# Delta rule of a hybrid transformer block: another way to the triangular inverse, norms by column groups, and work moved between stages

## The chip, the cores and the metric

One core of a Trainium2 chip runs the whole kernel in one launch. The metric is device time in microseconds (us), the median of the runs; for the kernel before it is 1261.51 us over three runs (1257.89 to 1262.75). Engines: PE is the matrix engine (TensorE), DVE the vector engine, ACT the scalar engine, POOL is GpSimd, SP issues the DMAs. They run side by side and wait for each other through semaphores, all written by hand here.

## The reference, cut to what matters

Four layers run one after another: forgetting attention, a gated delta net with a convolutional FFN behind each, then latent attention and block attention. The change concerns the delta net, and there the part between its input projections and its output projection (8 heads of width 128, 272 tokens padded to 3 chunks of C = 96):

```python
q = l2norm(q) * (Dh ** -0.5); k = l2norm(k)
dec = jnp.exp(jnp.where(incl, gc[..., :, None] - gc[..., None, :], -jnp.inf))
A = jnp.where(strict, (kc @ kc.T) * dec * beta, 0.0)
sol = lax.linalg.triangular_solve(A + I, rhs, lower=True, unit_diagonal=True)   # rhs: keys, values
qk = (qc @ kc.T) * dec
def step(S, xs):                      # over the 3 chunks
    U = U0_n - W_n @ S
    O = qd_n @ S + qk_n @ U
    S = gl_n * S + U.T @ kd_n
O = rmsnorm(O, o_gain) * silu(og);  out = O @ w_out
```

The kernel doesn't solve: it builds the inverse D of I + A (96 x 96, lower triangular, one for each of 24 head and chunk pairs) and multiplies by it.

## The kernel before, in words

Weights are split in a high and a low part, and every big product is three matmuls at float32r (L365 to L367). The delta net has these stages.

- Projections (`project`, L1393): for each head d four features, q, k, v and gate. ACT scales them out of PSUM (`tap`), DVE adds three convolution taps (`conv`, L1736), ACT applies silu and squares (`silu_sq`). A `head_sum` (L1387) behind a later feature adds the squares over the 128 rows with one float32 matmul of 272 columns. ACT and DVE also split the next weights (L346, L351).
- Gap: behind the last feature PE turns the gates (L1454), makes the last two head sums, and turns the values of four heads (`turn_values`, L1427), while ACT takes the root (L1678) and DVE the reciprocal (L1786).
- Preparation, head by head: `spread` (L1410 to L1420) lays norms and decays over the rows, DVE normalises k and q (L1802, L1805), `prepare` makes k k' (L1435), k q' (L1441) and turned keys (L1446). DVE makes `a_tr` (L1814), `qd_all` (L1819) and `qk_all` (L1821). POOL masks the next-to-diagonal pairs out of `a_tr` (L1927). For heads 4 to 7 `turn_values` stands in this loop.
- Start of the inverse: DVE writes identity minus pairs (L1842), PE turns it (L1491).
- Levels: blocks of 2, 4, ... 64 are joined in pairs, six levels of 8 heads, 48 units. A unit n is `x_of(n)` (A times D, L1475), a masked copy on DVE (L1851), `update(n)` (D times that, L1483), a subtraction on DVE (L1856) and `turn(n)` (L1491) with a copy on ACT (L1697). Every product is 3 matmuls of 96 x 96 by 96 columns in float32, which the trace shows as 6 instructions. The last level isn't turned.
- Recurrence over the chunks (L1520 to L1545), squares (L1509), output norm, output projection.

The order on every engine is the order in which the loops of `dn_pe`, `dn_act`, `dn_dve` and `dn_pool` are written; nothing reorders it.

Of the kernel before, what the change touches and what calls it, by code (L numbers as in the profile page):

```python
# [13 lines left out]
P = 128  # L14
# [9 lines left out]
DNH = 8  # L24
# [5 lines left out]
LEVELS = 7  # L30
ROWS = 40
# [13 lines left out]
def tables():  # L45
# [30 lines left out]
    def causal(blocks):  # L76
        parts = []
        for q0, q1 in blocks:
# [10 lines left out]
           for b in (1 << n for n in range(1, LEVELS))]  # L89
    t["levels"] = np.concatenate(lev, 1)  # L90
    t["pairs"] = ((i == j + 1) & (j % 2 == 0)) * 1.0
    t["ident_c"] = np.eye(C)
    t["one_of"] = np.tile(np.arange(2 * ROWS) == ROWS, (P, 1)) * 1.0
# [7 lines left out]
    sin = np.concatenate([-sin[0:16], sin[16:32]], 0)  # L101
    t["mla_q"] = np.concatenate([np.concatenate([plain, cos, sin], 0), np.concatenate([cos, sin, plain], 0)], 1)
    return t
# [65 lines left out]
def build(nc, x, table, params, w, out):  # L169
# [7 lines left out]
    with ctx:  # L177
# [49 lines left out]
        def pr(name):  # L227
# [66 lines left out]
        sel_r = put("sel_r", [DNH, P], dtype=F32R)  # L294
        put.at += 4 * DNH * (TP - P)
        a_tr = put("a_tr", [DNH, TP], C)
        kn_all, qd_all = put("kn_all", [DNH, TP]), put("qd_all", [DNH, TP])
        qk_all = put("qk_all", [DNH, TP], C)
        put.at -= 4 * DNH * TP
        v_all = put("v_all", [DNH, TP])  # L300
        vb_all = put("vb_all", [DNH, NC, P], C)
# [16 lines left out]
        q_st, e_row, dec = put_x("q_st", [2, TP]), put_x("e_row", [2, TP]), put_x("dec", [2, TP], C)  # L318
        put_x.at -= 3 * 4 * 2 * TP
        s_t = put_x("s_t", [DNH, P])  # L320
        r_st, u_st = put_x("r_st", [2, P], C), put_x("u_st", [2, P], C)
        o_gate = m

# [6 lines left out]
            "osq", "osum", "oroot", "ohi", "olo", "oinv", "onorm", "ospread", "zero", "pads", "bgt_out", "eg", "ot")}  # L330
# [39 lines left out]
        def _(sp):  # L370
# [5 lines left out]
            for name, kind, n in STREAM:  # L376
# [11 lines left out]
                if name == "w_dn_out":  # L388
                    sp.wait_ge(dn["ssq"], 2 * DNH)
                    sp.dma_start(q_sq[:, 0:SEQ], table[:, kept:kept + SEQ]).then_inc(mla_in, 16)  # L390
                    sp.dma_start(k_sq[:, 0:SEQ], table[:, kept + SEQ:]).then_inc(mla_in, 16)
# [91 lines left out]
        def keep_clock(count):  # L483
            for _ in range(count):
                nc.tensor.matmul(bank[0][:, 0:2 * P], ones_r, fixed_r[:, 0:2 * P], start=True, stop=True)  # L485
# [886 lines left out]
        GAP_HEADS = 4  # L1372

        O_SPREAD = [(0, 0)] + [(4, n * width(TAIL)) for n in range(DNH - 1)]

# [3 lines left out]
        def dn_pe(pe):  # L1379
# [7 lines left out]
            def head_sum(d, which):  # L1387
                pos = d + 32 * which
                pe.wait_ge(dn["sq"], 2 * d + which + 1)
                nc.tensor.matmul(bank[7][0:ROWS, 0:T], tb("one_of")[:, ROWS - pos:2 * ROWS - pos], (q_sq, k_sq)[which][:, 0:T],  # L1390
                                 start=d == 0 and which == 0, stop=d == DNH - 1 and which == 1).then_inc(dn["ssq"], 1)

            def project(d):  # L1393
                for which in range(4):
                    if which == 3:
                        pe.wait_ge(dn["gate"], d) if d else pe.wait_ge(dn["raw"], 2)
                    elif d >= 2:
                        pe.wait_ge(dn["conv"], 3 * (d - 2) + which + 1)
                    feature(d, which)
                    if d and which < 2:  # L1400
                        head_sum(d - 1, which)

            def spread(h):
                if h == 0:
                    pe.wait_ge(dn["inv"], 4)
                    pe.wait_ge(dn["rows"], 2)
                    pe.wait_ge(dn["fixed"], 2)
                wait(pe, dn["qn"], h)
                wait(pe, dn["kn"], h)
                nc.tensor.matmul(bank[1][:, 0:T], sel_r[:, h, :], inv_r[:, 1, :], start=True, stop=True).then_inc(dn["bk"], 1)  # L1410
                nc.tensor.matmul(bank[0][:, 0:T], sel_r[:, h, :], inv_r[:, 0, :], start=True, stop=True).then_inc(dn["bq"], 1)
                wait(pe, dn["dec"], h)
# [9 lines left out]
            def turn_values(h):  # L1422
                wait(pe, dn["vt_out"], h)
                if h >= GAP_HEADS:
                    pe.wait_ge(dn["kt_out"], NC * h)
                for c in range(NC):
                    mm = nc.tensor.transpose(bank[2][0:C, c * P:(c + 1) * P], v_all[:, h, c * C:(c + 1) * C], ident)  # L1427
                mm.then_inc(dn["vt"], 1)

            def prepare(h):  # L1430
                pe.wait_ge(dn["kn"], h + 1)
                wait(pe, dn["at"], h)
                for c in range(NC):
                    cc = slice(c * C, (c + 1) * C)
                    mm = nc.tensor.matmul(bank[6][0:C, cc], kn_all[:, h, cc], kn_all[:, h, cc], start=True, stop=True)  # L1435
                mm.then_inc(dn["kk"], 1)
                pe.wait_ge(dn["qn"], h + 1)
                wait(pe, dn["qk"], h)
                for c in range(NC):
                    cc = slice(c * C, (c + 1) * C)  # L1440
                    mm = nc.tensor.matmul(bank[7][0:C, cc], kn_all[:, h, cc], q_st[:, h % 2, cc], start=True, stop=True)  # L1441
                mm.then_inc(dn["qq"], 1)
                pe.wait_ge(dn["vt_out"], max(h + 1, GAP_HEADS))
# [3 lines left out]
                mm.then_inc(dn["kt"], 1)  # L1447
            small_pe(pe, "w_beta_a", bank[3][:, 0:T], 64)
            for d in range(DNH):
                project(d)  # L1450
            pe.wait_ge(dn["conv"], 3 * (DNH - 1))
            pe.wait_ge(dn["bg"], 2)
            for c in range(NC):
                mm = nc.tensor.transpose(bank[1][0:C, c * 64:(c + 1) * 64], bg[0:64, c * C:(c + 1) * C], ident[0:64, 0:64])  # L1454
            mm.then_inc(dn["bgt"], 1)
            for which in range(2):
                head_sum(DNH - 1, which)
            for h in range(GAP_HEADS):
                turn_values(h)
            pe.wait_ge(dn["bgt_out"], 1)  # L1460
            spread(0)
            for h in range(DNH):
                if h + 1 < DNH:
                    spread(h + 1)
                if h >= GAP_HEADS:
                    turn_values(h)
                prepare(h)
            pe.wait_ge(dn["kt_out"], NC * DNH)

            def x_of(n):  # L1470
                pe.wait_ge(dn["d_in"], n - DNH + 1)
                wait(pe, dn["x_out"], n - DNH - 1)
                for c in range(NC):
                    cc = slice(c * C, (c + 1) * C)
                    mm = nc.tensor.matmul(bank[n % 2][0:C, cc], a_tr[:, n % DNH, cc], d_in[:, n % DNH, cc], start=True, stop=True)  # L1475
                mm.then_inc(dn["x"], 1)

            def update(n):
                pe.wait_ge(dn["x_out"], n - DNH + 1)
                pe.wait_ge(dn["d"], n - 1)  # L1480
                for c in range(NC):
                    cc = slice(c * C, (c + 1) * C)
                    mm = nc.tensor.matmul(bank[2 + n % 2][0:C, cc], x_slot(n)[:, cc], d_tr[:, n % DNH, cc], start=True, stop=True)  # L1483
                mm.then_inc(dn["dd"], 1)

            def turn(n):
                pe.wait_ge(dn["d"], n + 1)
                wait(pe, dn["d_in"], n - 1)
                for c in range(NC):
                    cc = slice(c * C, (c + 1) * C)  # L1490
                    mm = nc.tensor.transpose(bank[4 + n % 2][0:C, cc], d_tr[:, n % DNH, cc], ident[0:C, 0:C])  # L1491
                mm.then_inc(dn["t"], 1)
            for n in range(LEVELS * DNH + 3):
                if DNH <= n < LEVELS * DNH:
                    x_of(n)
                if DNH <= n - 1 < LEVELS * DNH:
                    update(n - 1)
                back = n - (0 if n < DNH else 2)
                if n < DNH or DNH <= back < (LEVELS - 1) * DNH:
                    turn(back)  # L1500

            def squares(hd):
# [4 lines left out]
                for g in range(GROUPS):  # L1507
                    at = TAIL[0] + g * n_t
                    mm = nc.tensor.matmul(bank[6][ROW * g:ROW * (g + 1), 0:n_t], tb("one_of")[:, ROWS - hd:ROWS - hd + ROW],  # L1509
                                          sq[:, hd % 2, at:at + n_t], start=hd == 0, stop=hd == DNH - 1)  # L1510
                mm.then_inc(dn["osum"], 1)
            for c in range(NC):
# [10 lines left out]
                def second_half(hd):  # L1523
# [4 lines left out]
                    else:  # L1528
                        rhs = vb_all[:, hd, 0, :]
                        if hd == 0:  # L1530
                            pe.wait_ge(dn["d"], LEVELS * DNH)
                    wait(pe, dn["u_out"], g - 1)
# [58 lines left out]
        def dn_act(act, st):  # L1591
# [18 lines left out]
            def project(d):  # L1610
                after = following("w_dn", d)
                tap(d, 0, qd_all)
# [661 lines left out]
```

## Time and profile before

| | us |
|---|---|
| median of three runs | 1261.51 |
| the profiled execution, its own time | 1262.73 |
| its span, first to last instruction | 1260.7 |
| mean granted clock of PE, share of 2.4 GHz | 0.978 |

The span is cut by what PE does: projections of the delta net until 549.5 us, gap until 561.75, preparation until `a_tr` of the last head ends at 582.73, start of the inverse until 590.51, levels until 651.97, recurrence and norm until 684.27, then the output projection. "x6" in a row counts instructions of the trace, two for each float32 matmul.

### The profile page before, as it was taken

Reading aid. Unit: us, or ns where it says so; the run is one execution under the profiler, and the core shown is the slowest. Engines: PE = TensorE matmul, PEld = TensorE weight load, DVE = VectorE, ACT = ScalarE, POOL = GpSimd, SP = SyncE. Lnnn points to the kernel's source line nnn. Section 1 sums busy time; section 2 is a strip of 40 time slices with the busy share of each in tenths; the row PEclk is TensorE's granted clock in tenths of the full one; section 3 lists DMA queues with packets and bytes.
Section 4 is the critical chain, followed back from the end, with each engine's and each line's share of the span. In section 5 each row is a group of like instructions: output and inputs, shape, how many; then the busy total and the mean of one; then the engine's idle time right before and its main releaser. Section 6 shows DMA issues by size and latency. Waiting matters only on the chain.

```text
span 1260.7 us, 27818 instructions
## 1 busy us (share of the span) xinstructions
PE 1195.9 (95%) x10201; PEld 1121.5 (89%) x10201; DVE 864.8 (69%) x1691; ACT 709.8 (56%) x1478; POOL 61.8 (5%) x69
## 2 busy tenths in 40 slices
PE   5999998999999899988999899999999999899996
PEld 5888877999999799977998799999988999899995
DVE  5888865777754577766444577885466786778874
ACT  6677664666644467654225566665455655655543
POOL 0000000121100000002000011210000000000000
PEclk9999998999999999988998999999999999999998
DMA  7433314455555255530000436566634343444431
GB/s 260 125 128 102 126 60 130 129 171 171 169 172 159 77 188 150 163 111 2 2 2 2 134 101 187 179 178 180 179 114 148 120 148 120 134 145 139 133 117 35
DMA packets 49977, 160.35 MB, mean 127 GB/s; under 512 B 5488, under 2 KB 8432, under 8 KB 49776
## 3 DMA queue, kind: packets, MB, share of 16 engines
q1 hardware_dynamic: 49904, 159.35, 40.9%
q8 instruction: 49, 0.80, 0.3%
q14 instruction: 24, 0.20, 0.0%
HBM read 158.28 MB, written 1.05 MB: 126 GB/s over the span
## 4 chain that ended last, share of the span: by engine, by line
PE 86%; DVE 7%; ACT 5%; issue 2%; DMA 0%; SPq 0%; ACTq 0%; DVEq 0%
PE banks L365 23%; PE banks L367 21%; PE banks L366 21%; PE banks L1475 2%; PE banks L1483 2%; ACT w_hi L346 2%; PE banks L902 2%; PE banks L438 1%; DVE w_lo L351 1%; PE banks L882 1%; PE banks L867 1%; DVE m L518 1%; PE banks L1491 1%; PE banks L485 1%; DVE t_sin L1131 1%
## 5 line engine op out<-in xcount | busy, mean ns | idle before, releaser
L351 DVE TENSOR_TENSOR w_lo<-raw,w_hi 128x1024 fp32r<-128x1024 f32 (+5 forms) x332 | 370.4, 1122 | 195.4 <-ACT w_hi L346 194.4
L365 PE MATMUL banks<-x_hi,w_hi 128*128 128x272 f32 (+2 forms) x1624 | 476.8, 294 | 8.0 <-DVE x_lo L498 3.9
L367 PE MATMUL banks<-x_hi,w_lo 128*128 128x272 f32 (+2 forms) x1624 | 464.2, 286 | 0.0
L366 PE MATMUL banks<-x_lo,w_hi 128*128 128x272 f32 (+2 forms) x1624 | 464.0, 286 | 0.0
L346 ACT ACTIVATE w_hi<-raw 128x1024 fp32r<-128x1024 f32 (+5 forms) x332 | 314.4, 955 | 92.2 <-PE banks L367 87.4
L365 PEld LDWEIGHTS banks<-x_hi,w_hi 128*128 128x128 f32 x1624 | 307.2, 189 | 25.6 <-issue 15.3
L366 PEld LDWEIGHTS banks<-x_lo,w_hi 128*128 128x128 f32 x1624 | 307.9, 190 | 0.1
L367 PEld LDWEIGHTS banks<-x_hi,w_lo 128*128 128x128 f32 x1624 | 307.3, 189 | 0.0
L365 PE MATMUL banks<-hid_hi,w_hi 128*128 128x272 f32 (+1 forms) x352 | 101.3, 288 | 0.0
L367 PE MATMUL banks<-hid_hi,w_lo 128*128 128x272 f32 (+1 forms) x352 | 100.3, 285 | 0.0
L366 PE MATMUL banks<-hid_lo,w_hi 128*128 128x272 f32 (+1 forms) x352 | 99.9, 284 | 0.0
L1007 ACT ACTIVATE p_e<-s_m,mx 128x128 f32<-128x128 f32 (+3 forms) x112 | 48.0, 429 | 70.3 <-DVE mx L1111 70.3
L365 PE MATMUL banks<-o_hi,w_hi 128*128 128x256 f32 (+2 forms) x256 | 77.9, 304 | 6.7 <-DVE w_lo L351 5.5
L1366 POOL TENSOR_TENSOR hid<-g_e,u_y 128x272 f32<-128x272 f32 (+1 forms) x44 | 48.9, 1111 | 530.2 <-ACT g_e L1310 530.2
L366 PE MATMUL banks<-o_lo,w_hi 128*128 128x256 f32 (+2 forms) x256 | 74.4, 291 | 0.0
L367 PE MATMUL banks<-o_hi,w_lo 128*128 128x256 f32 (+2 forms) x256 | 74.3, 290 | 0.0
L1335 DVE SCALAR_TENSOR_TENSOR g_y<-banks,par,g_y 128x271 f32<-128x271 f32 (+1 forms) x88 | 43.3, 492 | 43.1 <-ACT u_y L1303 37.5
L365 PEld LDWEIGHTS banks<-hid_hi,w_hi 128*128 128x128 f32 x352 | 66.3, 188 | 1.1
L366 PEld LDWEIGHTS banks<-hid_lo,w_hi 128*128 128x128 f32 x352 | 66.2, 188 | 0.0
L367 PEld LDWEIGHTS banks<-hid_hi,w_lo 128*128 128x128 f32 x352 | 66.1, 188 | 0.0
L365 PEld LDWEIGHTS banks<-o_hi,w_hi 128*128 128x128 f32 x256 | 50.2, 196 | 10.4 <-issue 4.4
L366 PEld LDWEIGHTS banks<-o_lo,w_hi 128*128 128x128 f32 x256 | 50.2, 196 | 0.2
(288 smaller groups left out, 1820.7 us busy)
## 6 DMA issues: line engine op xcount, KB each, us to landing
raw<-w_up SPq DMA_DIRECT2D x88, 512.0 KB, 4.4
raw<-w_attn SPq DMA_DIRECT2D x32, 512.0 KB, 4.6
raw<-w_dn SPq DMA_DIRECT2D x32, 512.0 KB, 4.0
raw<-w_moba SPq DMA_DIRECT2D x32, 512.0 KB, 3.9
raw<-w_down SPq DMA_DIRECT2D x32, 384.0 KB, 3.2
raw<-w_down SPq DMA_DIRECT2D x32, 320.0 KB, 3.2
raw<-w_mla SPq DMA_DIRECT2D x16, 384.0 KB, 3.2
raw<-w_attn_out SPq DMA_DIRECT2D x8, 512.0 KB, 4.2
```

The lines of the kernel that those rows point to most:

```text
L346: nc.scalar.activation(w_hi[:, q, 0:wd], raw[:, q, 0:wd], ACT.Copy).then_inc(hi_done, 1)
L351: nc.vector.tensor_tensor(w_lo[:, q, 0:wd], raw[:, q, 0:wd], w_hi[:, q, 0:wd].bitcast(F32), ALU.subtract).then_inc(lo_done, 1)
L365: nc.tensor.matmul(dst, hi, src[0][:, k, c0:c1], start=first, stop=False)
L366: nc.tensor.matmul(dst, hi, src[1][:, k, c0:c1], start=False, stop=False)
L367: return nc.tensor.matmul(dst, lo, src[0][:, k, c0:c1], start=False, stop=last)
L438: mm = nc.tensor.matmul(bank[where][ROW * g:ROW * (g + 1), 0:n_t], ones[:, 0:ROW], sq[:, slot, at:at + n_t], start=first, stop=last)
L902: mm = nc.tensor.matmul(bank[5][64 * hh:64 * hh + 64, d0:d1], v_s[r, b, 64 * hh:64 * hh + 64], probs, start=i == 0, stop=i == len(part) - 1)
L1007: ins = nc.scalar.activation(p_e[r, hh, s0:s1], s_m[r, hh, s0:s1], ACT.Exp, bias=mx[r, hh, b:b + 1], scale=SCALE[f], accum_out=rs[r, hh, b ...
L1335: ins = nc.vector.scalar_tensor_tensor(y[:, r, lo:T], bank[2 * r + half][:, lo - back:T - back], conv_w(f, j, half, 2 - back), y[:, r, lo: ...
L1366: nc.gpsimd.tensor_tensor(hid[:, r, o0:T], g_e[:, r, o0:T], u_y[:, r, o0:T], ALU.mult).then_inc(prod_ready, 1)
L1475: mm = nc.tensor.matmul(bank[n % 2][0:C, cc], a_tr[:, n % DNH, cc], d_in[:, n % DNH, cc], start=True, stop=True)
L1483: mm = nc.tensor.matmul(bank[2 + n % 2][0:C, cc], x_slot(n)[:, cc], d_tr[:, n % DNH, cc], start=True, stop=True)
```

## The change

- Substitution: within blocks of 8 (`BASE`) the inverse is made by DVE for all 24 pairs at once. POOL masks the blocks of 8 out of `a_tr`, PE packs them into 8 columns each (`compact`, 3 matmuls of 8 columns per head), ACT copies the 192 columns (`low`), 7 matmuls with `row_from` (a table that comes by its own DMA) spread the rows, and DVE runs 7 steps of a product and a subtraction. 8 instructions write the blocks back to 96 x 96 (`d_in`), and PE turns these. 30 matmuls that nobody reads (`keep_clock`) stand between.
- Levels: `LEVELS` is 5, so 4 levels of joining (32 units) are left. Levels 1 and 2 (to 16, to 32) use whole 96 x 96 products. Levels 3 and 4 (`PARTS`: 32 with 32, 64 with 32) use the sub-blocks alone. `update` comes two units behind `x_of`, `turn` three.
- k k' and k q' are one product of 192 columns into two banks (`kq_psum`), from `kq_all`, which holds k and q side by side.
- Norms: `head_sum` is 4 matmuls of 68 columns into 4 row groups of a bank, so that root and reciprocal work on 128 x 68. The last two head sums and the decays of head 0 stand ahead of the last feature; the gates are turned during head 6.
- All eight `turn_values`, their copies, the last two weight splits and the last two silus stand within the inverse.

```diff
             def head_sum(d, which):
-                nc.tensor.matmul(bank[7][0:ROWS, 0:T], tb("one_of")[...], (q_sq, k_sq)[which][:, 0:T], ...)
+                for g in range(GROUPS):
+                    mm = nc.tensor.matmul(bank[7][ROW * g:ROW * (g + 1), 0:n_t], tb("two_of")[:, ROW - pos:2 * ROW - pos],
+                                          (q_sq, k_sq)[which][:, g * n_t:(g + 1) * n_t], ...)
...
+                    if d == DNH - 1 and which == 3:
+                        head_sum(d, 0)
+                        head_sum(d, 1)
+                        pe.wait_ge(dn["conv"], 3 * d + 2)
+                        spread_decay(0)
...
+                    mm = nc.tensor.matmul(kq_psum[:, c, 0:2 * C], kn_all[:, h, cc], kq_all[:, h, :, cc], start=True, stop=True)
...
+            def compact(h):
+                pe.wait_ge(dn["pair"], h + 1)
+                for c in range(NC):
+                    n = (h * NC + c) * BASE
+                    mm = nc.tensor.matmul(bank[3][0:C, n:n + BASE], x_st[:, h % 4, c * C:(c + 1) * C], tb("own_place"), ...)
...
+            for k in range(BASE - 1, 0, -1):
+                nc.tensor.matmul(bank[ROW_BANK[k - 1]][0:C, 0:DNH * NC * k], row_from[:, (k - 1) * C:k * C],
+                                 by_block(low)[:, :, 0:k], start=True, stop=True).then_inc(dn["rows8"], 1)
+            keep_clock(30, 3)
...
+                    if part:
+                        lo, hi = part
+                        mm = nc.tensor.matmul(sub(bank[n % 2][hi], c, lo), sub(a_tr[lo, n % DNH, :], c, hi),
+                                              sub(d_in[lo, n % DNH, :], c, lo), start=True, stop=True)
...
             def project(d):                                  # ACT, last head
+                if last:
+                    silu_sq(d, 1, kn_all, k_sq)
+                    st(nc.scalar.activation(prime_out[:], eps["rms"], ACT.Sqrt))
+                    tap(d, 2, v_all)
+                    norm_root()
+                    exp_gates()
+                    act.wait_ge(chunk_used, chunk("w_dn", d, 3) + 1)
+                    decays(0)
...
+            for k in range(BASE - 1, 0, -1):                 # DVE
+                dve.wait_ge(dn["rows8"], BASE - k)
+                st(nc.vector.tensor_tensor(part3[:, :, 0:k], inv3[:, :, k:k + 1].to_broadcast([C, DNH * NC, k]), row, ALU.mult))
+                st.settle()
+                st(nc.vector.tensor_tensor(inv3[:, :, 0:k], inv3[:, :, 0:k], part3[:, :, 0:k], ALU.subtract))
+                st.settle()
```

First place: PE behind the third feature of the last head. Before, the fourth feature (L365 to L367) ends here, and then come:

```order
L367 MATMUL banks<-x_hi,w_lo 128x272
L1454 MATMUL banks<-tab,bg 96x64 x3
L1390 MATMUL banks<-q_sq,tab 40x272
L1390 MATMUL banks<-k_sq,tab 40x272
L1427 MATMUL banks<-tab,v_all 96x128 x12
L1410 MATMUL banks<-inv_r,sel_r 128x272
```

Now, the end of the third feature, and ahead of the fourth (L378 to L380):

```order
L380 MATMUL banks<-x_hi,w_lo 128x272
L1412 MATMUL banks<-q_sq,tab 32x68 x4
L1412 MATMUL banks<-k_sq,tab 32x68 x4
L1459 MATMUL banks<-rows_d,fixed_r 96x288
L1462 MATMUL banks<-gc_neg_r,rows_d 96x96 x3
L1463 MATMUL banks<-later_r,ident_r 96x288
L1465 MATMUL banks<-rows_d,fixed_r 128x288
L378 MATMUL banks<-x_hi,w_hi 128x272
```

Head sums and the decays of head 0 moved ahead of a feature; the twelve turns of values left.

Second place: PE from the last head's preparation into the inverse. Before (L1491 is `turn`, L1475 `x_of`, L1483 `update`):

```order
L1427 MATMUL banks<-tab,v_all 96x128 x3
L1435 MATMUL banks<-kn_all 96x96 x3
L1441 MATMUL banks<-q_st,kn_all 96x96 x3
L1446 MATMUL banks<-tab,kn_all 96x128 x3
L1491 MATMUL banks<-tab,d_tr 96x96 x24
L1475 MATMUL banks<-d_in,a_tr 96x96 x6
```

Now (L1485 is the joined product, L1497 `compact`, L1519 the rows, L500 `keep_clock`, L1557 `turn`, L1534 `x_of`):

```order
L1485 MATMUL banks<-kq_all 96x192 x3
L1489 MATMUL banks<-tab,kq_all 96x128 x3
L1497 MATMUL banks<-tab,x_st 96x8 x6
L1519 MATMUL banks<-q_raw,sq 96x168
L1519 MATMUL banks<-q_raw,sq 96x144
L1519 MATMUL banks<-q_raw,sq 96x120
L1519 MATMUL banks<-q_raw,sq 96x96
L1519 MATMUL banks<-q_raw,sq 96x72
L1519 MATMUL banks<-q_raw,sq 96x48
L1519 MATMUL banks<-q_raw,sq 96x24
L500 MATMUL banks<-fixed_r 128x256 x30
L1557 MATMUL banks<-tab,d_in 96x96 x24
```

Two short products, seven row products and the unread matmuls stand where PE went to the turns at once.

Third place: PE in the level that joins 32 with 32, two units of it (L1531 and L1545 are `x_of` and `update` on sub-blocks, L1472 `turn_values`):

```order
L1531 MATMUL banks<-d_in,a_tr 32x32 x3
L1545 MATMUL banks<-d_tr,x_st 32x32 x3
L1557 MATMUL banks<-tab,d_tr 96x96 x3
L1472 MATMUL banks<-tab,v_all 96x128 x3
L1531 MATMUL banks<-d_in,a_tr 32x32 x3
L1545 MATMUL banks<-d_tr,x_st 32x32 x3
L1557 MATMUL banks<-tab,d_tr 96x96 x3
```

The two products of a unit shrank, the turn stayed whole, and in every third unit the turns of one head's values follow.

## Rows read from the trace of the kernel before

**Rows 1.** The profile's page: the span and the engines' busy time.

```profile
span 1260.7 us, 27818 instructions
PE 1195.9 (95%) x10201; PEld 1121.5 (89%) x10201; DVE 864.8 (69%) x1691; ACT 709.8 (56%) x1478; POOL 61.8 (5%) x69
```

**Rows 2.** Stretches of the span by stage; the first line names the columns.

```profile
core 0: us, PE busy (x) PEld busy (x) DVE busy (x) ACT busy (x) POOL busy (x), PEclk, DMA share, GB/s
444.90:549.50 104.60, 104.60 (x778) 96.33 (x777) 77.80 (x114) 70.80 (x119) 0.55 (x1) 1.00 0.50 154
549.50:561.75 12.25, 7.64 (x36) 5.53 (x36) 6.70 (x12) 7.55 (x15) 0.12 (x1) 0.67 0.58 194
561.75:582.73 20.98, 19.47 (x181) 18.40 (x180) 15.49 (x51) 14.11 (x46) 3.83 (x4) 0.95 0.00 1
582.73:590.51 7.78, 4.01 (x27) 2.87 (x27) 6.17 (x11) 3.62 (x10) 4.87 (x6) 0.83 0.00 1
590.51:651.97 61.46, 61.12 (x696) 60.80 (x695) 28.12 (x96) 11.65 (x41) 2.30 (x4) 0.97 0.01 2
651.97:684.27 32.30, 29.19 (x328) 26.17 (x328) 14.69 (x45) 18.81 (x60) 0.00 (x0) 0.99 0.01 2
```

**Rows 3.** Chain of waits (start, us, what): a head sum, squares in four groups.

```profile
542.73 0.58 PE banks L1390 x2
...
674.70 0.25 PE banks L1509 x8
```

**Rows 4.** Instructions in time order (start, busy us), last head and output norm.

```profile
543.95 1.05 ACT L346 ACTIVATE w_hi<-raw 128x1024 fp32r<-128x1024 f32 x1
547.39 0.43 ACT L1608 ACTIVATE k_sq<-kn_all 128x272 f32<-128x272 f32 x1
550.91 1.28 ACT L1676 ACT_TABLE_LOAD   x1
547.08 1.56 DVE L1736 SCALAR_TENSOR_TENSOR v_all<-banks,par,v_all 128x271 f32<-128x271 f32 x3 [0.82 <-ACT v_all L1600]
680.69 0.57 DVE L1887 RECIPROCAL rstd<-root 128x65 f32<-128x65 f32 x1 [2.04 <-ACT root L1719]
559.02 0.17 DVE L1798 TENSOR_SCALAR nbz<-eg_t 96x24 f32<-96x24 f32 x1 [2.71 <-ACT eg_t L1684]
```

**Rows 5.** Instructions in time order, preparation: PE, then DVE and POOL.

```profile
568.58 0.37 PE L1410 MATMUL banks<-inv_r,sel_r 128*128 128x272 f32 x1
569.57 0.67 PE L1435 MATMUL banks<-kn_all 128*96 128x96 f32 x6
567.54 0.43 DVE L1805 SCALAR_TENSOR_TENSOR q_st<-qd_all,banks 128x272 f32<-128x272 f32 x1
568.03 0.76 DVE L1814 SCALAR_TENSOR_TENSOR a_tr<-banks,bg_t,dec 96x96 f32<-96x96 f32 x3
568.71 0.45 DVE L1819 TENSOR_TENSOR qd_all<-q_st,e_row 128x288 f32<-128x288 f32 x1
569.08 0.45 DVE L1821 TENSOR_TENSOR qk_all<-banks,dec 96x288 f32<-96x288 f32 x1
569.45 0.42 DVE L1802 TENSOR_TENSOR kn_all<-kn_all,banks 128x272 f32<-128x272 f32 x1
563.80 0.95 POOL L1927 TENSOR_TENSOR x_st<-a_tr,tab 96x288 f32<-96x288 f32 x1 [14.09 <-DVE a_tr L1814]
```

**Rows 6.** L1842: duration ns min/median/max, first and last start.

```profile
L1842 DVE TENSOR_TENSOR d_tr<-tab,x_st x8: 443/748/1047, 583.8 to 588.8; 96x288 f32<-96x288 f32 x8
```

**Rows 7.** Chain of waits in the levels and at their end.

```profile
643.25 0.25 PE banks L1491 x3
643.50 0.51 PE banks L1475 x6
644.01 0.51 PE banks L1483 x6
...
651.71 0.26 DVE d_tr L1856
```

More of the change, by code:

```diff
@@ L29 @@
 SLOTS = 3
-LEVELS = 7
-ROWS = 40
+LEVELS = 5
+BASE = 8
+HALF = 16
 CHUNK = 8 * P
@@ L101, in tables @@
     sin = np.concatenate([-sin[0:16], sin[16:32]], 0)
+    late = np.concatenate([(j == i // BASE * BASE + k) * 1.0 for k in range(1, BASE)], 1)
     t["mla_q"] = np.concatenate([np.concatenate([plain, cos, sin], 0), np.concatenate([cos, sin, plain], 0)], 1)
+    t["row_from"] = late
     return t
@@ L1431, in prepare @@
                 pe.wait_ge(dn["kn"], h + 1)
+                pe.wait_ge(dn["qn"], h + 1)
+                if h == 0:
+                    pe.wait_ge(dn["conv"], 3 * DNH)
+                    pe.wait_ge(dn["root"], 1)
                 wait(pe, dn["at"], h)
[L1433 to L1437, printed above, removed]
                 wait(pe, dn["qk"], h)
@@ L1447, in prepare @@
                 mm.then_inc(dn["kt"], 1)
+            def compact(h):
+                pe.wait_ge(dn["pair"], h + 1)
+                if h == 0:
+                    pe.wait_ge(dn["gate"], DNH)
+                for c in range(NC):
+                    n = (h * NC + c) * BASE
+                    mm = nc.tensor.matmul(bank[3][0:C, n:n + BASE], x_st[:, h % 4, c * C:(c + 1) * C], tb("own_place"),
+                                          start=True, stop=True)
+                mm.then_inc(dn["block"], 1)
             small_pe(pe, "w_beta_a", bank[3][:, 0:T], 64)
@@ L1450, in dn_pe @@
                 project(d)
[L1451 to L1461, printed above, removed]
+            spread_norm(0)
             for h in range(DNH):
                 if h + 1 < DNH:
-                    spread(h + 1)
-                if h >= GAP_HEADS:
-                    turn_values(h)
+                    spread_norm(h + 1)
+                    spread_decay(h + 1)
                 prepare(h)
+                if h:
+                    compact(h - 1)
             pe.wait_ge(dn["kt_out"], NC * DNH)
+            pe.wait_ge(dn["at"], DNH)
+            pe.wait_ge(dn["qk"], DNH)
+            compact(DNH - 1)
+            pe.wait_ge(dn["low"], 1)
+            pe.wait_ge(dn["from"], 16)
+            for k in range(BASE - 1, 0, -1):
+                nc.tensor.matmul(bank[ROW_BANK[k - 1]][0:C, 0:DNH * NC * k], row_from[:, (k - 1) * C:k * C],
+                                 by_block(low)[:, :, 0:k], start=True, stop=True).then_inc(dn["rows8"], 1)
+            keep_clock(30, 3)
             def x_of(n):
@@ L1845, in dn_dve @@
+            for n in range(DNH, LEVELS * DNH + 2):
                 if n < LEVELS * DNH:
                     lv = n // DNH
[L1847 removed]
+                    dve.wait_ge(dn["clear"], min(lv, LEVELS - 3))
                     wait(dve, dn["dd"], n - DNH - 1)
                     dve.wait_ge(dn["x"], n - DNH + 1)
[L1850 to L1852 removed]
```

278 lines of the change are left out of this document (181 added, 97 removed).

## The prediction

> **What bounds the kernel now.** The page comes first: PE is busy for 95% of the span and no other engine for more than 69% [rows 1]. An average over stages says little, so the stretches are read next [rows 2]. In the projections PE is busy for all of 104.6 us, at a granted clock of 1.00 (2.4 GHz). There any PE time taken out is time won. In the gap of 12.25 us PE has 7.64 us of work, and the clock is 0.67, so part of it ran at 1.2 GHz. In the preparation (20.98 us) PE has 19.47 and DVE 15.49. At the start of the inverse (7.78 us) PE has 4.01 and DVE 6.17. In the levels PE is busy for 61.12 of 61.46 us, DVE for 28.12 and ACT for 11.65: the levels are bound by PE alone, and the chain shows the unit, 0.51 + 0.51 + 0.25 = 1.27 us, 40 times, and 8 units of 1.02 us without a turn [rows 7]. That makes 59 us; the rest up to 61.46 is the first units at the lower clock and the last latency. So the stretch to look at is the 61 us of levels, then the gap.
>
> **The change part by part**, each with its gain or cost against the profiled execution.
>
> Head sums, projections. One costs 0.58 us of the chain as 2 instructions of 272 columns. The squares before the output norm are the same kind in four groups, 65 columns each, and 8 instructions take 0.25 us [rows 3]. Fourteen stand within the projections, and PE bounds these: 14 x 0.33 = 4.6 us gained. At the least I take half of the difference, 2.3. The selectors, now two DVE instructions at heads 1 and 2, lie beside PE: DVE is busy for 77.8 of 104.6 us [rows 2].
>
> From the head sum at 542.73 (of head 6, ahead of the last head's third feature) to the first product of the preparation, 19.02 us before (561.75). Now, step by step: head sum and third feature (24 matmuls at 104.60 / 778 = 0.134 us, so 3.2) end at 546.5. The squares of the keys, for which the last head sums wait, come from ACT: the split that starts at 543.95 takes 1.05, then silu and square 0.9, so 545.9 [rows 4]. That is just in time. Two head sums 0.5 and the decays 0.8 (0.99 for the whole spread, 568.58 to 569.57 [rows 5], less two matmuls) put the last feature at 547.8 to 551.0. Beside it ACT loads the root's table (1.28 and 0.2, to 547.4), scales v (0.4) and takes the root of 68 columns (0.35): 548.2. DVE then needs 0.57 for the reciprocal of 65 columns [rows 4], about 0.2 each for two short operations, 0.45 for a product of 272 columns: 549.8. The values' convolution stands next in DVE's queue, 1.56 [rows 4]: 551.4. Only then k and q of head 0 are normalised, 0.7 [rows 5]: 552.1. The spread of head 1 waits for this and takes 1.0, so the first product starts at 553.1. Gain 19.02 - 10.4 = 8.6 us. What was in the gap (first split, table, four turned values with their copies) is hidden beside the feature or in the levels. Bounds: 10 if the convolution comes before the root; 6.5 if the keys' squares are a microsecond late and everything behind them.
>
> Preparation. Before, DVE's round of a head without values is 2.25 us: 567.54 to 569.45, and 0.34 for the keys that start there (0.42 with its end overlapped) [rows 5]; the four with values then share the rest, (20.98 - 4 x 2.25) / 4 = 3.0 each. Now one product of 192 columns must be over before DVE can start `a_tr`, and the next cannot start until `qk_all` has left the two banks. The loop is: `qk_all` start to end 0.45, product 6 x 0.17 = 1.04 (0.085 us per 96 columns [rows 7]) and 0.2 to arrive, `a_tr` 0.68 (568.03 to 568.71), `qd_all` 0.37 [rows 5]: 2.75. PE has 0.99 + 1.04 + 0.25 for the keys and the 6 instructions of `compact`. Those have 8 columns but the same 96 x 96 weights; a turn of 96 columns costs 0.25 for 3 [rows 7], so up to 0.5, at least 6 x 0.031 = 0.19 [rows 3]. I take 0.5, since the weights are whole: 2.78. I take 2.8 per head: 1.24 + 7 x 2.8 + 0.76 = 21.6, against 20.98: 0.6 lost. Bounds: DVE's own 2.25 per head would gain 3.3; 3.0 would lose 2.0.
>
> Start of the inverse, counted from the end of the last `a_tr` (582.73 before), 7.78 us before. Now: POOL masks, 0.95 [rows 5], `compact` 0.5 and 0.2 to arrive, ACT's copy of 192 columns 0.45, the first row product 0.3 and 0.2: 2.65. DVE then works 14 operations, each waiting for the one before. One of 24 columns takes 0.17 (L1798 [rows 4]), one of 288 takes 0.45 [rows 5], so one costs 0.15 and a nanosecond per column, and 0.03 for the wait: 14 x 0.18 + 2 x 672 columns = 3.9. Then 8 expansions of 288 columns, 0.37 apart: 3.05, the last turn 0.3. Sum 9.9: 2.1 lost. The 30 unread matmuls (some 3.5 us) lie beside DVE's steps. Bounds: 1 lost if the steps go at 0.2 flat; 6 lost if they cost 0.45 each.
>
> The expansions rest on a row that spreads: the same size took 443 to 1047 ns, while POOL worked [rows 6]; now POOL has nothing then, hence the lower end. By the Trainium skill, GPSIMD Engine Reference, section "1. Specifications", GpSimd shares its SBUF interfaces with VectorE and the two contend when a DVE instruction reads two SBUF inputs. With such contention the sum would have 8 x 0.6 = 4.8 us more; `qd_all`, with two SBUF inputs beside POOL, kept its 0.45 [rows 5], so the trace doesn't bear it out everywhere.
>
> Levels. 16 whole units of 1.27: 20.3. Five heads' values turned there, 0.25 each: 1.25. In level 3 the two products have 32 rows, 32 weights' columns and 32 columns. What such an instruction costs, no row shows: 0.031 us if they pass as in the squares [rows 3], 0.085 if as whole ones [rows 7]. I take 0.04, near the lower, since the weights and the columns are both as short there: 0.24 + 0.24 + 0.25 = 0.73 a unit, 5.8; two whole updates of the level before add 0.5, three heads' values 0.75. Level 4 at 64 columns: 0.055, 0.33 + 0.33: 8 x 0.66 = 5.3, with 3 turns 0.75 and the last latency (arrive, DVE copy, update, DVE 0.26) 1.6. Sum 20.3 + 1.25 + 7.1 + 7.7 = 36.3 against 61.46: 25.1 gained. DVE's share of a short unit, two operations of 96 columns, is 0.4 to 0.5, ACT's 0.3 and a third of 0.48: both stay under PE. The two weight splits (1.05 on ACT, 1.2 on DVE) fall into whole units, of which DVE uses less than half [rows 2]; the silus lie beside DVE's steps. If that cover were gone, they would cost their own 5 us.
>
> Sum: -4.6 - 8.6 + 0.6 + 2.1 - 25.1 = -35.6. The profiled execution took 1262.73, so 1227.1. It stands 1.2 us above the median of the runs; the median should be 1226.
>
> **Rivals.**
> - Short products cost as much as whole ones (0.085). For it: the rows that show 0.031 spread over four column groups, and here three products in a row use the same corner. Against it: weights and columns are a third. Price (0.51 - 0.24) x 2 x 8 + (0.51 - 0.33) x 2 x 8 = 7.2: 1233.
> - The round between PE, DVE and ACT sets the pace of the short units, not PE. For it: in order queues, four handovers a unit; against: two and three units of slack. If each short unit took 1.27 as a whole one: 16 x 1.27 - 5.8 - 5.3 = 9.2: 1235.
> - The clock falls. Where PE was busy for half of a stretch, 4.01 of 7.78 us, the granted clock fell to 0.83, and the levels began at 1.2 GHz (0.97 on average, so about 3.7 of 61.46 us at half) [rows 2]. If it falls in the turns of the start or in the short units, some 5 us more: 1231.
> - The preparation reaches DVE's bound, 2.25 a head: 1222.
> - The other side: the clock falls at DVE's steps and stays at 1.2 GHz until the output norm. Then each us of PE work from there costs another: 34 in the levels and 25 in the recurrence, 59 us, so 1285. It decides from 36 us of such work on. Against it: the clock came back within the first units before, and stood at 0.99 in the recurrence [rows 2].
>
> By the Trainium skill, TensorE: Matmul & The Clock Gate, the section "Wait — 56ns, not 53.3ns?", the sequencer can spend about 62 ns on each matmul however short it is. That rule would be the mechanism of the first rival, in part: 0.37 for 6 instructions instead of 0.24 would add 0.13 x 16 + 0.04 x 16 = 2.7 us. The trace has 8 instructions in 0.25 us, 31 ns each [rows 3], so it doesn't hold for those.
>
> **How the numbers follow.** Forecast 0.58, short products dear 0.15, handovers 0.07, clock 0.10, preparation faster 0.07, clock lost throughout 0.02; the last 0.01 is for several losses that meet. Likeliest 1226. All lower bounds together (1.5 in the gap, 4 in the preparation, 1 at the start, 2 in the levels) would reach 1217, the dear rivals with one upper bound 1240: the range 1217 to 1240 leaves out less than 2 in 10, and takes in the bounds. 0.5% is 6 us, about what a measurement of this kernel can tell from no change; all cases but the last two lie beyond it: faster 0.96, within 0.01, slower 0.03.
>
> **What would show it.** Right: 14 head sums at 0.25 us; no PE idleness over 2 us between the last feature and the first joined product; joined products about 2.8 us apart; some 10 us from the last `a_tr` to the first `x_of`; whole units at 1.27, short ones near 0.7; clock at 1.00 in levels and recurrence. Wrong: short products near 0.5 us for three, DVE steps over 0.3 us each, joined products nearer 2.3 or above 3 us, or a recurrence longer than 32.3 us.

## The result

The changed kernel takes 1240.68 us (median of 4 runs, 1238.13 to 1245.05), the kernel before 1260.45 beside it: ratio 0.984, 95% interval 0.9821 to 0.986. That is 20 us less, where 35 were forecast, and just outside the range (1217 to 1240). The profiled execution is the one of 1245.05. Its page, to be laid beside [rows 1]:

```profile
span 1243.3 us, 27522 instructions
PE 1183.2 (95%) x10101; PEld 1112.5 (89%) x10101; DVE 854.2 (69%) x1673; ACT 707.2 (57%) x1465; POOL 58.2 (5%) x64
```

Shares of busy time are the same as before. Nothing on the page tells a good forecast from a missed one; the stretches do. They have the columns of [rows 2], and a few overlap: 575.80 to 584.20 lies within the start of the inverse, the two last within the recurrence.

```profile
441.40:541.65 100.25, 98.94 (x840) 95.03 (x844) 80.28 (x115) 70.44 (x118) 0.00 (x0) 1.00 0.54 169
541.65:551.67 10.02, 8.95 (x88) 8.38 (x89) 6.90 (x15) 7.72 (x16) 0.34 (x1) 1.00 0.49 152
551.67:573.69 22.02, 20.62 (x164) 19.36 (x162) 15.60 (x52) 12.92 (x44) 5.85 (x7) 1.00 0.00 1
573.69:587.60 13.91, 11.51 (x75) 10.81 (x76) 7.60 (x26) 5.03 (x13) 1.93 (x3) 0.75 0.01 2
575.80:584.20 8.40, 8.38 (x47) 8.38 (x48) 6.64 (x22) 2.01 (x3) 0.75 (x2) 0.59 0.01 4
587.60:608.98 21.38, 20.93 (x238) 20.28 (x237) 9.95 (x32) 8.15 (x21) 0.00 (x0) 1.00 0.17 51
608.98:616.89 7.91, 7.82 (x128) 6.28 (x128) 3.86 (x17) 3.30 (x10) 0.00 (x0) 1.00 0.01 2
616.89:628.11 11.22, 10.65 (x121) 8.85 (x121) 5.48 (x19) 1.47 (x5) 0.00 (x0) 0.82 0.01 2
628.11:664.53 36.42, 35.71 (x264) 33.14 (x264) 13.19 (x40) 18.35 (x58) 0.00 (x0) 0.73 0.01 2
634.00:640.00 6.00, 5.99 (x29) 5.64 (x28) 1.86 (x7) 2.25 (x8) 0.00 (x0) 0.50 0.00 0
648.00:653.00 5.00, 4.96 (x44) 4.75 (x43) 2.35 (x8) 2.65 (x9) 0.00 (x0) 1.00 0.00 0
```

Against the forecast, term by term, in us of the two profiled executions:

| term | forecast | measured | from |
|---|---|---|---|
| head sums in the projections | -4.6 | -3.4 | first to that of 541.65: 81.77, before 85.22 |
| last head sums to first joined product | -8.6 | -9.0 | 10.02, before 19.02 |
| preparation | +0.6 | +1.0 | 22.02, before 20.98 |
| start of the inverse | +2.1 | +6.1 | 13.91, before 7.78 |
| levels | -25.1 | -21.0 | 40.51, before 61.46 |
| recurrence, to the root of the output norm | 0 | +8.1 | 36.42, before 28.3 |
| elsewhere | 0 | +0.8 | +2.4 ahead of the first head sum, -1.6 behind the root |
| sum | -35.6 | -17.4 | spans: 1243.3 - 1260.7 |

The 2.4 us ahead of the first head sum are not the change's: the first instruction of that head sum starts at 457.44 before and at 459.81 here, and anywhere from 455.31 to 458.97 in the twelve variants below, which all leave the code ahead of it alone. Three terms miss, and the largest stands in a part that the change does not touch: the 264 instructions of the recurrence take 8 us more. The last two rows show why: the granted clock was 0.50 (1.2 GHz), 29 instructions in 6 us, and later 1.00 (2.4 GHz), 44 in 5 us.

The chain of waits (start, us, what) answers to [rows 3] and [rows 7]. A head sum; the gap; then one round of the preparation and the start of the next:

```profile
538.18 0.26 PE banks L1412 x8
...
542.86 0.97 ACT w_hi L359
543.83 0.42 ACT kq_all L1674
...
544.72 1.28 ACT L1691
...
546.49 0.32 ACT root L1711
...
546.83 0.59 DVE rstd L1891
...
557.44 1.11 PE banks L1485 x6
558.55 0.33 PE banks L1489 x3
558.88 0.43 PE banks L1497 x6
...
560.31 0.78 PE banks L1485 x4
...
573.77 0.85 POOL x_st L2069
574.62 0.14 issue
574.76 0.66 PE banks L1497 x6
575.42 0.02 issue
575.44 0.34 ACT q_raw L1784
575.77 0.04 issue
575.82 2.44 PE banks L1519 x14
578.26 5.90 PE banks L500 x30
584.16 0.27 PE banks L1557 x3
...
608.98 0.30 PE banks L1531 x6
...
613.00 0.09 PE banks L1545 x3
613.09 0.38 PE banks L1557 x3
...
613.86 0.38 PE banks L1557 x3
...
622.59 0.45 PE banks L1531 x6
623.04 0.46 PE banks L1545 x6
...
624.53 0.78 PE banks L1531 x6
625.31 0.79 PE banks L1545 x6
```

The head sum is 0.26, joined products are 2.87 apart. From 578.26 to 584.16 the chain is nothing but the 30 unread matmuls (L500), 0.197 us each on average: their starts are 0.213 apart while the clock is at 0.50, and 0.117 apart at the end, when it is back. A unit of level 3 takes 0.77 (613.09 to 613.86). In level 4 two products take 0.45 and 0.46, and from 624.5 the same two take 0.78 and 0.79: there the clock fell. DVE in the same stretch, in time order:

```profile
576.45 0.33 DVE L1947 TENSOR_TENSOR th<-k_raw,banks 96x168 f32<-96x168 f32 x1 [1.81 <-PE banks L1519]
...
580.31 0.20 DVE L1949 TENSOR_TENSOR k_raw<-k_raw,th 96x24 f32<-96x24 f32 x1
580.54 3.04 DVE L1955 TENSOR_TENSOR d_in<-k_raw,tab 96x288 f32<-96x288 f32 x8
```

Fourteen steps in 4.1 us, then 8 expansions in 3.04. The first expansion was ready at about 580.9, and the turn that needs it started at 584.16.

### The profile page after: what moved, and what is told of

It reads as the page before. It is cut to its first block, busy times and chain, and to the rows that moved or that the text cites. A ratio compares the mean times of both kernels' runs of the same rounds, so it can differ in the third digit from the quotient of the medians.

```text
span 1243.3 us, 27522 instructions
## 1 busy us (share of the span) xinstructions
PE 1183.2 (95%) x10101; PEld 1112.5 (89%) x10101; DVE 854.2 (69%) x1673; ACT 707.2 (57%) x1465; POOL 58.2 (5%) x64
## 4 chain that ended last, share of the span: by engine, by line
PE 88%; DVE 5%; ACT 4%; issue 1%; DMA 1%; SPq 0%; POOL 0%; ACTq 0%; DVEq 0%
PE banks L378 24%; PE banks L380 22%; PE banks L379 22%; PE banks L500 2%; PE banks L917 2%; ACT w_hi L359 2%; PE banks L453 1%; PE banks L897 1%; DVE w_lo L364 1%; PE banks L882 1%; DVE m L533 1%; PE banks L1557 1%; PE banks L879 1%; PE banks L1602 1%; PE banks L1485 1%
## 5 line engine op out<-in xcount | busy, mean ns | idle before, releaser
L378 PE MATMUL banks<-x_hi,w_hi 128*128 128x272 f32 (+2 forms) x1624 | 477.7, 294 | 7.1 <-DVE x_lo L513 3.4
L380 PE MATMUL banks<-x_hi,w_lo 128*128 128x272 f32 (+2 forms) x1624 | 464.4, 286 | 0.0
L378 PEld LDWEIGHTS banks<-x_hi,w_hi 128*128 128x128 f32 x1624 | 307.4, 189 | 19.1 <-issue 9.1
L380 PEld LDWEIGHTS banks<-x_hi,w_lo 128*128 128x128 f32 x1624 | 307.7, 189 | 0.0
L378 PE MATMUL banks<-hid_hi,w_hi 128*128 128x272 f32 (+1 forms) x352 | 101.3, 288 | 0.0
L380 PE MATMUL banks<-hid_hi,w_lo 128*128 128x272 f32 (+1 forms) x352 | 99.8, 284 | 0.0
L378 PE MATMUL banks<-o_hi,w_hi 128*128 128x256 f32 (+2 forms) x256 | 77.3, 302 | 6.7 <-DVE w_lo L364 5.5
L380 PE MATMUL banks<-o_hi,w_lo 128*128 128x256 f32 (+2 forms) x256 | 73.8, 288 | 0.0
L1350 DVE SCALAR_TENSOR_TENSOR g_y<-banks,par,g_y 128x271 f32<-128x271 f32 (+1 forms) x88 | 43.3, 492 | 44.2 <-ACT u_y L1318 38.5
L378 PEld LDWEIGHTS banks<-hid_hi,w_hi 128*128 128x128 f32 x352 | 66.1, 188 | 1.1
L380 PEld LDWEIGHTS banks<-hid_hi,w_lo 128*128 128x128 f32 x352 | 66.1, 188 | 0.0
L378 PEld LDWEIGHTS banks<-o_hi,w_hi 128*128 128x128 f32 x256 | 49.7, 194 | 10.5 <-issue 4.4
```

The costliest lines, as they stand in the source:

```text
L378: nc.tensor.matmul(dst, hi, src[0][:, k, c0:c1], start=first, stop=False)
L380: return nc.tensor.matmul(dst, lo, src[0][:, k, c0:c1], start=False, stop=last)
L1350: ins = nc.vector.scalar_tensor_tensor(y[:, r, lo:T], bank[2 * r + half][:, lo - back:T - back], conv_w(f, j, half, 2 - back), y[:, r, lo: ...
```

## The experiments

Each variant starts from the changed kernel. Stages in us, from one profiled execution each; "fell" is where the granted clock went to 0.50 in the levels and "back" where it returned. Ratios are against the kernel before, measured beside each (1260.45 to 1260.89 us).

| kernel | prep. | start | levels | recurr. | fell, back | time | ratio, 95% interval |
|---|---|---|---|---|---|---|---|
| the change | 22.0 | 13.9 | 40.5 | 36.4 | 624, 648 | 1240.68 | 0.984, 0.9821 to 0.986 |
| keep0 | 22.0 | 12.2 | 42.3 | 33.3 | 621, 638 | 1239.53 | 0.9833, 0.9817 to 0.985 |
| keep12 | 22.0 | 11.4 | 49.4 | 35.3 | 611, 648 | 1243.59 | 0.9857, 0.9834 to 0.9879 |
| x_whole | 22.0 | 13.9 | 44.3 | 34.6 | 624, 644 | 1243.78 | 0.987, 0.9852 to 0.9887 |
| hold1 | 22.0 | 12.4 | 45.1 | 33.4 | 621, 641 | 1243.3 | 0.9861, 0.9845 to 0.9878 |
| fill | 22.0 | 11.6 | 45.0 | 35.3 | 623, 647 | 1240.94 | 0.9843, 0.9806 to 0.988 |
| whole34 | 22.0 | 14.0 | 43.3 | 28.1 | no | 1237.72 | 0.9823, 0.9806 to 0.984 |
| whole_fill | 22.0 | 11.6 | 45.1 | 28.1 | no | 1235.28 | 0.981, 0.9787 to 0.9833 |
| part3 | 22.0 | 14.0 | 40.2 | 28.1 | no | 1232.05 | 0.9778, 0.976 to 0.9796 |
| part3_keep0 | 22.0 | 12.2 | 41.9 | 28.1 | no | 1233.55 | 0.9779, 0.976 to 0.9798 |
| part3_fill2 | 22.0 | 11.1 | 40.2 | 28.1 | no | 1229.94 | 0.976, 0.9743 to 0.9776 |
| split3 | 19.5 | 11.0 | 40.2 | 28.1 | no | 1228.38 | 0.9752, 0.9729 to 0.9775 |
| best | 19.6 | 11.3 | 40.2 | 28.1 | no | 1229.23 | 0.9746, 0.9731 to 0.9761 |

**The unread matmuls.** keep0 takes the 30 out, keep12 leaves 12.

```
-            keep_clock(30, 3)          (keep0)
...
-            keep_clock(30, 3)
+            keep_clock(12, 3)          (keep12)
```

> The change without the 30 unread matmuls behind the row products. Theory Q (they stand in PE's queue ahead of the eight turns and, at 1.2 GHz, last 5.9 us, 3.1 us longer than DVE's steps to the first expansion): first turn some 3 us earlier, start of the inverse about 10.5 us instead of 14.1; but the first whole units then run at 1.2 GHz as before the change, which gives back 2 to 3. Net 0.5 to 1.5 us faster than the change (ratio to before 0.983). Theory R (they only fill time that DVE sets): the start keeps 14 us and the levels lose 2 to 3 us at the lower clock, ratio 0.986.

> The change with 12 unread matmuls instead of 30. Theory Q: at 1.2 GHz they last 2.4 us and end before the first expansion, so the start is 10.5 us, 3.5 less than with 30; if the clock comes back with 12 as with 30 the net is 3.5 us faster than the change (ratio 0.981), if not, as with none. Theory R: start stays at 14 us.

Both starts are shorter (12.2 and 11.4 against 13.9), as they would be if the queue of unread matmuls stood in front of the turns. How much of the difference is the queue's is less sure: hold1 below leaves this stretch as it is in the change, and its start took 12.4, since its clock was at 0.50 for 3.4 us of it and not for 6.8. keep0 gives 1.7 us back in levels that begin at 1.2 GHz, and its time is that of the change within the interval. keep12 lost the clock in level 3 already, 29.5 us after the levels began, where the change lost it after 36.5; why there, is open.

**Shape or activity.** x_whole computes `x_of` whole in levels 3 and 4; hold1 keeps the short products and puts one unread matmul behind each unit.

```
-                part = part_of(n)      (x_whole, in x_of)
+                part = None
...
+                if n >= (LEVELS - 2) * DNH:      (hold1, behind turn_values)
+                    at, need = (6, 5) if n < 29 else (7, 6) if n < 32 else (6, 7)
+                    pe.wait_ge(dn["vt_out"], need)
+                    keep_clock(1, at)
```

> The change with x_of in levels 3 and 4 as whole 96 x 96 products again (one part of the change undone; the copies and the updates stay on sub-blocks). Theory C (the clock falls because of the short products and the recurrence then runs at 1.2 GHz until 648 us): levels 3 and 4 cost 16 x about 0.15 = 2 us more, but the clock stays at 1.00 and the recurrence takes 32.3 us as before instead of 40.4, net 5 us faster than the change. Theory L (the recurrence is slower because of something else in the change, such as the interleaved store of k and q): recurrence stays at 40 us and the kernel is 2 to 3 us slower than the change.

> The change with one unread matmul of 256 columns behind each unit of levels 3 and 4 (18 in all). Theory C: they cost 18 x 0.11 = 2 us and keep the clock at 1.00, the recurrence takes 32.3 us instead of 40.4: 6 us faster than the change (ratio 0.979). Theory L: 2 us slower, recurrence still 40 us.

Neither holds the clock: it falls at 624 and 621, in level 4, and the levels are 3.8 and 4.6 us longer. So half of the products whole is not enough, and one unread matmul a unit is not. Neither theory of the two expectations came out as it stands: the clock did not hold, and the times, which are those of theory L, go with a recurrence at the low clock (34.6 and 33.4 us), not with another cause.

**Both levels whole.** The sub-blocks go, the new start of the inverse and everything else stays; POOL clears and DVE masks as in the levels before.

```
-        PARTS = {LEVELS - 2: (slice(0, 32), slice(32, 64)), LEVELS - 1: (slice(0, 64), slice(64, 96))}
+        PARTS = {}
```

> The change with levels 3 and 4 undone to whole 96 x 96 products, masks and copies as in the kernel before (substitution, joined product, norms and moved work stay). Theory C (short products let the clock fall, and the recurrence pays): levels 24 x 1.27 + 8 x 1.02 + 8 x 0.33 for the values + 1.1 = 42.4 us against 40.5 in the change's profile, clock 1.00 through levels and recurrence, recurrence to the root of the output norm 28.3 us as before the change instead of 36.4: some 6 us faster than the change (ratio 0.979). Theory L (recurrence slower for another reason): 2 us slower, recurrence stays at 33 to 36. Theory S (the clock fell because 30 unread matmuls or the start upset it, not the short products): clock falls here too.

The two stretches of whole34, levels and recurrence:

```profile
585.30:628.60 43.30, 42.26 (x484) 41.50 (x481) 17.95 (x66) 12.99 (x36) 1.15 (x2) 1.00 0.09 26
628.60:656.70 28.10, 26.96 (x264) 24.26 (x264) 12.77 (x40) 17.62 (x58) 0.00 (x0) 1.00 0.01 2
```

The clock is 1.00 in both and the same 264 instructions take 28.10 us instead of 36.42. The recurrence, its layout and its operands are those of the change, so its 8 us were the clock and nothing else. The levels pay 2.8 us for it. The whole kernel is 3 us faster in the median (1237.72 against 1240.68), half of what was expected, and the intervals of the ratios overlap; the reading rests on the two stretches.

**Which level.** part3 keeps the 32-row sub-blocks of level 3 and makes level 4 alone whole.

```
+        PARTS = {LEVELS - 2: (slice(0, 32), slice(32, 64))}
```

> The change with level 4 alone undone to whole products; level 3 stays on sub-blocks. Theory C: level 3 takes 7.9 us, level 4 about 9.5 instead of 11.2 (its short products cost 0.91 a unit and the half clock 1.5); whole products behind the short ones keep or restore the clock before the recurrence: 5 to 8 us faster than the change (ratio 0.978 to 0.98), best of the two. If level 3 alone is enough to let the clock fall, the fall comes in level 4 (whole products at 1.2 GHz, 2 us a unit) and it is no faster than the change. Theory L: same as the change.

Its levels and recurrence, and a unit and a half of its level 4 in the chain:

```profile
583.70:623.90 40.20, 39.06 (x483) 36.45 (x481) 18.58 (x66) 12.93 (x36) 1.15 (x2) 1.00 0.09 28
623.90:652.00 28.10, 26.96 (x264) 24.27 (x264) 12.77 (x40) 17.61 (x58) 0.00 (x0) 1.00 0.01 2
```

```profile
618.49 0.51 PE banks L1548 x6
619.00 0.51 PE banks L1534 x6
619.50 0.51 PE banks L1548 x6
```

Level 4 whole costs 1.02 a unit against 0.91, and the levels as a whole are no longer than with it short (40.2 against 40.5), since they keep the clock. The 8.3 us of the recurrence come on top: 1232.05 against 1240.68, and the intervals of the ratios do not overlap. Only one execution of each kernel is profiled, but the mean granted clock of every run points the same way: 0.971 to 0.979 in the change, 0.982 to 0.987 in part3.

**Where the unread matmuls stand.** fill puts 8 behind the last preparation, 4 behind the last `compact` and 20 behind the rows; whole_fill does so with both levels whole.

```
+            keep_clock(8, 0)           (before the wait on kt_out)
...
+            keep_clock(4, 0)           (behind compact(DNH - 1))
...
-            keep_clock(30, 3)
+            keep_clock(20, 3)
```

> The change with the unread matmuls placed otherwise: 8 behind the last preparation, where PE waits for POOL, 4 behind the last compact, 20 instead of 30 behind the row products. Theory Q: the clock doesn't fall at the start, row products take 1.2 us instead of 2.4, the start 10 to 10.5 us instead of 13.9: 3.5 us faster than the change, the later fall of the clock stays (ratio 0.981). If the clock falls all the same the 20 last 4 us and the start is 12.

> Both of the above, whole products in levels 3 and 4 and the other places of the unread matmuls. Theories C and Q together: 10 us faster than the change, about 1230 us (ratio 0.976). If either falls, its part of the gain is missing.

The start is 11.6 in both, 2.3 us less, but the clock now falls later, around the turns (low from 582 to 592 in fill, 579 to 586 in whole_fill), and the levels give it back: 45.0 against 40.5, and 45.1 against 43.3. Against the change and against whole34, the intervals overlap.

**On top of part3.** split3 undoes the joined product, and with it DVE takes `qk_all` ahead of `qd_all`; part3_keep0 and part3_fill2 vary the unread matmuls again, now where the later stages keep the clock. part3_fill2 has 8, 4 and 28, and one behind each of the first 7 turns.

```
+                    mm = nc.tensor.matmul(bank[6][0:C, cc], kn_all[:, h, cc], kn_all[:, h, cc], ...)    (split3)
...
+                wait(pe, dn["qk"], h)
+                    mm = nc.tensor.matmul(bank[7][0:C, cc], kn_all[:, h, cc], qd_all[:, h, cc], ...)
...
-                    mm = nc.tensor.matmul(kq_psum[:, c, 0:2 * C], kn_all[:, h, cc], kq_all[:, h, :, cc], ...)
...
+                if n < DNH - 1:
+                    keep_clock(1, 3)   (part3_fill2, behind the turn)
```

> Level 4 whole (as in part3, ratio 0.9778) and the joined product undone: k k' and k q' are two products in two banks again, each with its own wait, and DVE takes qk_all before qd_all. Theory J (the joined product costs 2.87 us a head because DVE must wait for all of it and PE for the last read of both banks): a head goes at PE's own 2.7, the preparation takes 20.9 instead of 22.0 us, 1 us faster than part3. Rival: PE's instructions set the 2.87, then no change (ratio 0.978).

> Level 4 whole and no unread matmuls. With them part3 has a start of 14.0 us and full clock in the levels; without them, as in keep0, start 12.2 and the first units at 1.2 GHz, 1.7 us. Net same as part3, 1232 (ratio 0.977 to 0.979). If they are needed against a later fall of the clock, slower.

> Level 4 whole, 8 unread matmuls behind the last preparation, 4 behind the last compact, 28 behind the row products and one behind each of the first seven turns. Theory Q: the clock stays at 1.00 from the preparation to the levels (in fill it fell 4 us later, in the turns), start 11.2 us instead of 14.0, levels 40.2 as in part3: 2.5 to 3 us faster than part3, about 1229.5 (ratio 0.9755). If the clock falls in the turns all the same: start 12.5, levels 42, no gain.

split3's chain and two of its stretches, preparation and start:

```profile
556.97 0.51 PE banks L1484 x6
557.48 0.51 PE banks L1489 x6
557.99 0.33 PE banks L1493 x3
558.31 0.44 PE banks L1501 x6
...
559.76 0.51 PE banks L1484 x6
```

```profile
549.00:568.50 19.50, 19.50 (x209) 19.50 (x207) 18.50 (x52) 12.51 (x42) 5.54 (x7) 1.00 0.01 3
568.50:579.50 11.00, 9.36 (x81) 8.09 (x80) 7.91 (x26) 5.72 (x14) 1.88 (x3) 1.00 0.00 1
```

A head takes 2.79 (556.97 to 559.76) against 2.87, and PE has no idle time in it, where the change had 1.4 us in 22. Of the 2.5 us, 0.7 come in the first two rounds, 1.1 in the last one, which has no norm to spread and so leaves the joined form waiting for DVE (2.87 against 1.80 from product to product), 0.4 behind the last product and the rest in between. How much of this is the split and how much DVE's other order, no run tells apart. PE is busy to the last product, and the clock stays at 1.00 in the start, which then takes 11.0 with all 30 unread matmuls in place: at that clock they end at 575.85, just as the first expansion is there. In the median split3 is 3.7 us below part3 (1228.38 against 1232.05), but the intervals of the ratios overlap. part3_keep0 moves some 1.7 us from the start into the levels; its time is part3's within the interval. part3_fill2 keeps the clock in the start, 2.9 us less; its 1229.94 stands 2 us below part3, intervals overlapping.

best is split3 with part3_fill2's placement of the unread matmuls.

> Level 4 whole, two separate products in the preparation as in split3, and the unread matmuls placed as in part3_fill2. split3 in its profile already kept the clock at 1.00 through the start (11.0 us), so if that holds in every run the unread matmuls add nothing: 1228, as split3 (ratio 0.975). If split3's clock fell in some of its runs (its median is 1228.4 with one run at 1232.0), the placed ones steady it: 1226.5 to 1227.5, none above 1230 (ratio 0.974). A joined product would have cost 1.5 to 2.5 us of this.

It adds nothing that can be told from split3, which already had the clock. Both are some 12 us below the change and 31 to 33 below the kernel before.

## Why the prediction was right and wrong

The direction held, and the largest gain was where the forecast had put it. Three steps failed.

**The recurrence at 0 us, and the clock at 1.00 behind the short products.** This is the step that cost most: 8.1 us. The third rival ("If it falls in the turns of the start or in the short units, some 5 us more") named it and got a chance of 0.10. It was too cheap, since it stopped at the short units: the price is paid by whoever comes next. The last rival did carry a lost clock into the recurrence (25 us there), but had it fall at DVE's steps and stay down through all levels, and gave it 0.02. The forecast's own sign of being wrong, a recurrence and norm longer than 32.3 us, came: 40.4 (628.11 to 668.46). Short products are over soon, but the clock that they leave behind stays at 1.2 GHz for 20 us of the recurrence (to 648), with PE busy for 5.99 of 6.00 us. In the six profiles with level 4 on sub-blocks the clock fell in level 3 or 4 each time; in the seven with level 4 whole it stayed at 1.00 there, and the recurrence took 28.1. That "the clock came back within the first units before" was read from [rows 2] and does not carry over: in the six it came back only 13 to 20 us after the levels' end.

**"The 30 unread matmuls (some 3.5 us) lie beside DVE's steps".** They did not: they were counted at the full clock, and with the clock at 0.50 for most of them (0.213 each) they took 5.90 us, and stood in PE's own queue ahead of the turns. DVE's first expansion was there 3.2 us before the first turn began. Start 13.9 against 9.9. A shorter queue gave up to 2.5 us back (keep12), and so did the same queue at 2.4 GHz (split3, 11.0); of what is left to 9.9, most is the turns, which go at 1.0 us a pair with ACT's copies, where one turn of 0.3 had been counted.

**The size of level 4.** Forecast 0.66 a unit, measured 0.91 at the full clock: 0.076 us for each instruction on average, near the whole one's 0.085, not the 0.055 taken. The trace has the reason in the instructions' starts: within a product they are 0.055 to 0.059 apart behind the first, so the size taken was right, but from the last one to the first of the next product, on another sub-block, 0.146 to 0.148 pass. These 0.09 us at each change stand in no term of the forecast; whole products show none (all 0.085 apart in part3). The turns behind short products took 0.38 instead of 0.25 likewise. The rest up to 11.2 against 7.7, some 1.2 us, goes with the low clock at the end. So the first rival (short products as dear as whole ones) was nearly right in its price at 64 columns, for another reason, and untrue at 32: level 3's unit measured 0.77 against 0.73 forecast and 1.27 whole, and the level as a whole 7.9 against 7.1. By the Trainium skill, TensorE: Matmul & The Clock Gate, section "Wait — 56ns, not 53.3ns?", the sequencer spends about 62 ns on each matmul when the hardware's own decoding of them is off. Counted by the trace's instructions, the 12 of a level 3 unit would take 0.74 us, and they took 0.39 (0.77 less the turn). Counted by the program's matmuls, two instructions each, the 6 would take 0.37, and 0.39 agrees. No run here shows which count is meant, so the trace does not refute the page, and neither does the prediction's row of 8 instructions in 0.25 us, which are 4 such matmuls.

**Right.** The gap measured 10.0 against 10.4, on the forecast's own order: table load, root, reciprocal, and the values' convolution ahead of k and q of head 0. Whole units with their values' turns: 21.4 against 21.55. The handovers were no bound: level 3 ran at 0.77, not 1.27. DVE's steps 4.1 against 3.9, expansions 0.38 apart as forecast; POOL was busy for 0.75 us of that stretch, so the contention weighed there did not arise. The preparation 22.0 against 21.6, by the loop that was worked out: but splitting it again, with DVE's order changed, gained 2.5 us, so the joined form cost more than the 1.0 that the comparison with before gives (0.6 forecast), as the kernel before had work in that stretch that the change moved away. Head sums: 0.26 each as forecast, which is 4.2 over 13 intervals; 3.4 were gained there, and the remainder was not followed up.

**Still open.** What in the short units lets the clock go: one whole product or one unread matmul in each does not prevent it, level 4 whole does, and PE is recorded as busy for 10.65 of 11.22 us in the change. Nor do the runs show why keep12 lost it one level earlier. All six that lost it had level 3 on sub-blocks as well; level 4 on sub-blocks behind a whole level 3 was not tried, so it is not shown that level 4 does it by itself. Level 4 on sub-blocks with two or more unread matmuls a unit was not tried: at 0.12 us each (their starts in split3, at the full clock) one already costs what whole products do (1.02 - 0.91).

## What to carry to other kernels

Price a shortened stretch of PE together with the clock that it hands on: sub-blocks in level 4 saved 0.1 us a unit and, behind a level 3 on sub-blocks, cost the next stage 5 to 8 us. Price small products with what passes between them: here 0.09 us at each change to another sub-block, as much as an instruction and a half. Filler instructions on an in-order queue are cover only if they end before the work behind them is ready, and this must be reckoned at the low clock, at which they run when they are needed. Joining two products into one saves issues but makes both consumers and both operands wait for each other; where PE is the bound, check the wait first.

## What the runs showed of the hardware

- The granted clock fell to 0.50 while PE was recorded as busy: in hold1 PE was busy for all of 616 to 621, at 1.00, and for 18.96 us of 621 to 640, at 0.50. So in these rows PE's busy share alone does not tell what clock follows.
- Once down at the end of the levels, it stayed down for 17 to 37.5 us of busy work in these six profiles (keep0 the shortest, keep12 the longest).
- fp32 products on sub-blocks, one product after another: 0.050 us an instruction at 32 rows and columns (0.30 for 6), 0.076 with one side of 64 (0.45 or 0.46 for 6), 0.085 whole at 96. Within a product the starts are 0.031, 0.055 to 0.059 and 0.085 apart; the rest is some 0.09 us at each change of sub-block. Interleaved on two sub-blocks, 12 instructions of 32 took 0.39, 0.033 each.
- The unread matmuls of 256 columns start 0.213 us apart at a granted clock of 0.50 (the change) and 0.12 at 1.00 (split3).
